# A transformer block with retrieved experts: low parts on two engines in turn, selections cut in four lots, and projections, late rows and row requests reordered

## The reference, cut to what matters

```
px = modulate(rms_norm(x, norm1), sh1, sc1) @ w_in          # 8 chunks of 512 columns; the same for ctx (256 tokens)
x  = x + gt1 * (concat(neighbourhood_attention, hgrn2) @ w_out)
h  = modulate(rms_norm(x, norm2), sh2, sc2)
q  = (h @ wq).reshape(tokens, 8 heads, 2, 128)
s  = einsum(q, sub_keys)                                    # 128 scores for each head and half
s1, i1 = top_k(s[.., 0], 16); s2, i2 = top_k(s[.., 1], 16)
top, pos = top_k(s1[:, None] + s2[None, :], 16)             # the best 16 of 256 pairs
idx = i1 * 128 + i2 at pos;  g = softmax(top)
a   = gelu(u[idx] . h);  out = sum(g * a * v[idx])          # u, v: 16384 rows of 1024
x   = x + gt2 * out
```

## Time and profile before

| | |
|---|---|
| time, median of 3 runs | 2544.76 us (2541.76 to 2547.04) |
| the profiled execution | 2537.28 us, its span 2535.5 us |
| mean granted TensorE clock | 0.967 of full speed |
| PE busy | 2340.6 us, 92% of the span |
| DVE, ACT, POOL busy | 1758.0, 912.2, 620.9 us |
| HBM read, written | 432.60 MB, 52.43 MB |

### The profile page before, as it was taken

How to read it: one execution, slowest core, us unless ns; L and a number is a source line. 1 busy time by engine, 2 the same in 40 slices (tenths; PEclk the granted TensorE clock), 3 DMA queues, 4 the chain that set the end, 5 groups by cost and what they waited for, 6 DMA issues and landing times. The chain is left out here.

```text
span 2535.5 us, 31738 instructions
## 1 busy us (share of the span) xinstructions
PE 2340.6 (92%) x12435; PEld 2041.6 (81%) x12435; DVE 1758.0 (69%) x3152; ACT 912.2 (36%) x1192; POOL 620.9 (24%) x350
## 2 busy tenths in 40 slices
PE   7989888878998998899999799999999899999997
PEld 2768666753788898899999799999999576667775
DVE  6534676761588999799996677778786656654543
ACT  4212234221333233455553232333333434456323
POOL 0000032310344765533333333333330000000000
PEclk9989999889998999999999899999999999999999
DMA  7656310002225666788899999999995222112121
GB/s 258 219 180 207 140 50 1 1 17 100 75 98 192 217 223 205 243 307 324 320 341 360 344 361 354 353 355 353 357 354 188 85 84 66 50 42 67 62 96 67
DMA packets 178245, 489.22 MB, mean 193 GB/s; under 512 B 13712, under 2 KB 80400, under 8 KB 166576
## 3 DMA queue, kind: packets, MB, share of 16 engines
q1 hardware_dynamic: 141232, 352.95, 41.1%
q0 software_dynamic: 36864, 134.23, 13.8%
HBM read 432.60 MB, written 52.43 MB: 191 GB/s over the span
## 5 line engine op out<-in xcount | busy, mean ns | idle before, releaser
L1037 PE MATMUL ps<-h_high,u_high 128*128 128x384 f32 (+1 forms) x1152 | 403.2, 350 | 44.0 <-POOL u_low L1224 33.3
L1038 PE MATMUL ps<-h_low,u_high 128*128 128x384 f32 (+1 forms) x1152 | 396.0, 344 | 0.0
L1039 PE MATMUL ps<-h_high,u_low 128*128 128x384 f32 (+1 forms) x1152 | 395.8, 344 | 0.0
L1037 PE MATMUL ps<-w_high,v_high 128*128 128x384 f32 x1024 | 343.5, 335 | 18.3 <-DVE w_low L1603 18.3
L1038 PE MATMUL ps<-w_low,v_high 128*128 128x384 f32 x1024 | 342.7, 335 | 0.0
L1039 PE MATMUL ps<-w_high,v_low 128*128 128x384 f32 x1024 | 342.6, 335 | 0.0
L1037 PEld LDWEIGHTS ps<-h_high,u_high 128*128 128x128 f32 x1152 | 219.2, 190 | 55.5 <-POOL u_low L1224 36.2
L1037 PE MATMUL ps<-h_high,w_high 128*128 128x512 f32 x568 | 231.7, 408 | 32.0 <-DVE w_low L332 13.3
L1407 ACT ACTIVATE v_high<-v_raw 128x2048 fp32r<-128x2048 f32 x64 | 122.6, 1916 | 351.3 <-PE ps L1039 351.3
L1038 PE MATMUL ps<-h_low,w_high 128*128 128x512 f32 x568 | 225.4, 397 | 0.0
L1039 PE MATMUL ps<-h_high,w_low 128*128 128x512 f32 x568 | 224.7, 396 | 0.0
(11 more groups left out here) (405 smaller groups left out, 4571.8 us busy)
## 6 DMA issues: line engine op xcount, KB each, us to landing
v_raw<-in_peer_v SPq DMA_DIRECT2D x64, 1024.0 KB, 6.5
w_raw<-in_w SPq DMA_DIRECT2D x100, 512.0 KB, 3.5
u_first<-in_uT SPq DMA_DIRECT2D x32, 1024.0 KB, 6.1
u_second<-in_uT SPq DMA_DIRECT2D x32, 1024.0 KB, 6.2
xT<-in_late_w SPq DMA_DIRECT2D x56, 512.0 KB, 4.5
gelu_up<-gelu SPq DMA_DIRECT2D x128, 192.0 KB, 6.8
gates<-gates_sb SPq DMA_DIRECT2D x12, 2048.0 KB, 12.6
weighted<-gelu_up SPq DMA_DIRECT2D x64, 384.0 KB, 6.7
```

Source lines behind the costliest of these rows:

```text
L1037: pe.matmul(out, wh, mh, start=start, stop=False)
L1038: pe.matmul(out, wh, ml, start=False, stop=False)
L1039: return pe.matmul(out, wl, mh, start=False, stop=stop)
```

## The change

It has these parts:

1. Projections, late products: they are spread over steps 2 to 24 (`LATE_FIRST`, `LATE_PIECES`) where it was 0 to 26, two or three in a step, and on DVE stand at the end of their step.
2. The 32 moves of values go out four at a step in steps 12 to 19 (`MOVES`).
3. `high(2)` stands ahead of the row's sigmoid on ACT, `low(2)` ahead of the row's product on DVE.
4. The context scans of the two directions stand in steps 25 and 27, where they were in 25 and 26.
5. Experts, low parts: up to step 43 POOL makes those of even steps g, DVE those of odd steps, at the start of its step. POOL's subtraction stands ahead of the step's row requests and waits until DVE's of the step before is made.
6. `select` is cut in `best_keys`, `best_sums`, `best_pairs` and `key_numbers`. The first two run one step after the unit's scores, the other two a step later still, ahead of the first two of the next unit, and so do the shift, the row numbers and the second shift. ACT's first exponential moves from step 14 to 15.
7. Row requests of u: 44 lots in steps 16 to 43 (before 36), 62 in steps 44 to 67 (before 64), 22 in steps 68 to 75 (before 28). A lot's dot stands one step after its request throughout, where it was two for the first 36.

```diff
--- before.py
+++ after.py
@@ -198,11 +198,12 @@
                 eng.wait_ge(used, part_way[p])
 
 
-        late_pieces = at["in7"] - 1
+        LATE_FIRST, LATE_PIECES, MOVES = 2, 23, 8
 
         def late_at(p):
 
-            return range(min(p, late_pieces) * LATE // late_pieces, min(p + 1, late_pieces) * LATE // late_pieces)
+            first, end = (min(max(q - LATE_FIRST, 0), LATE_PIECES) * LATE // LATE_PIECES for q in (p, p + 1))
+            return range(first, end)
 
         def raw_of(p):
             return k.raws[:, p % RAW1, :] if p < NP - 2 else spare[:, p - NP + 2, :]
@@ -257,11 +258,12 @@
                     late_load(n)
                 if p == at["in6"]:
                     sp.wait_ge(evac, v_last)
-                    for c in range(NCB):
+                if at["in6"] <= p < at["in6"] + MOVES:
+                    first = (p - at["in6"]) * NCB * ROWS // MOVES
+                    for c, r in (divmod(x, ROWS) for x in range(first, first + NCB * ROWS // MOVES)):
                         k0 = min(max(QB * c - KB // 4, 0), GW - KB)
-                        for r in range(ROWS):
-                            sp.dma_start(k.vw[KB * (r % 4):KB * (r % 4) + KB, 2 * c + r // 4, :],
-                                         vnat[GW * (r % 2) + k0:GW * (r % 2) + k0 + KB, r // 2, :]).then_inc(moved, 16)
+                        sp.dma_start(k.vw[KB * (r % 4):KB * (r % 4) + KB, 2 * c + r // 4, :],
+                                     vnat[GW * (r % 2) + k0:GW * (r % 2) + k0 + KB, r // 2, :]).then_inc(moved, 16)
             sp.wait_ge(late_used, LATE)
             sp.dma_start(pred_f, k.dram["pred"].rearrange("p d s t -> p (d s t)")).then_inc(k.preds, 16)
             sp.dma_start(k.mask[:], k.dram["win_mask"]).then_inc(k.table_in, 16)
@@ -336,6 +338,7 @@
             h_lows(k.xT, h_high, h_low, 0, 0)
             low(1)
             h_lows(ctxT, hc_high, hc_low, 1, KT)
+            low(2)
             dve.wait_ge(sg_c, 2)
             dve.tensor_tensor(c_row, c_row, row_gate, ALU.mult).then_inc(silu_c, 1)
             dve.wait_ge(silu_c, 3)
@@ -378,9 +381,7 @@
 
             n = 0
             for p in range(NP):
-                for x in late_at(p):
-                    late_mod(x)
-                if p + 2 < NP:
+                if 2 < p + 2 < NP:
                     low(p + 2)
                 for j in ends[p]:
                     if jobs[j].kind == "silu":
@@ -397,9 +398,11 @@
                     forget_gates(0)
                 if p == f_last + 1:
                     forget_gates(1)
-                if f_last + 1 < p <= f_last + 3:
-                    context_scan(p - f_last - 2)
-                    context_keys(p - f_last - 2)
+                if p in (f_last + 2, f_last + 4):
+                    context_scan((p - f_last) // 2 - 1)
+                    context_keys((p - f_last) // 2 - 1)
+                for x in late_at(p):
+                    late_mod(x)
 
         @block.scalar
         def _(act):
@@ -440,11 +443,12 @@
                     act.wait_ge(scaled, KT * s + t + 1)
                     act.activation(h[:, t, :], y[:, t, :], ACT.Identity, scale=a1[:, t, s:s + 1],
                                    bias=m1[:, t, s:s + 1]).then_inc(modulated, 1)
+            high(2)
             act.wait_ge(rows_in, 16)
             act.activation(row_gate, c_row, ACT.Sigmoid).then_inc(sg_c, 1)
             n = 0
             for p in range(NP):
-                if p + 2 < NP:
+                if 2 < p + 2 < NP:
                     high(p + 2)
                 for j in ends[p]:
                     job = jobs[j]
@@ -1016,14 +1020,19 @@
     return OUT_G + 2 + 2 * u if u < 4 else OUT_G + 10 + 9 * (u - 4) // 4
 
 
+
 def pick_step(n):
 
-    return PICK_AT + 7 * n // 9 if n < 36 else SPREAD_AT + 3 * (n - 36) // 8 if n < 100 else 68 + 2 * (n - 100) // 7
+    if n < 44:
+        return PICK_AT + (SPREAD_AT - PICK_AT) * n // 44
+    if n < 106:
+        return SPREAD_AT + BATCHES // EXPERT_TILES * (n - 44) // 62
+    return GROUPS - 8 + 8 * (n - 106) // 22
 
 
 def dot_step(n):
 
-    return pick_step(n) + (2 if n < 36 else 1)
+    return pick_step(n) + 1
 
 
 def row_step(n):
@@ -1215,14 +1224,16 @@
                     .then_inc(row_in[total % RING], 16)
 
             for x in range(WQ_G + U_G):
+                if x + OUT_G < SPREAD_AT and x % 2 == 0:
+                    pool.wait_ge(u_hi, PIECES_BEFORE + x + 1)
+                    if x:
+                        pool.wait_ge(u_split, PIECES_BEFORE + x)
+                    pool.tensor_tensor(u_low[:, x % 2], u_raw[x % 2][:], u_high[:, x % 2].bitcast(F32),
+                                       ALU.subtract).then_inc(u_split, 1)
                 for n in picks_at[x + OUT_G]:
                     if n == 0:
                         pool.wait_ge(indexed, 1)
                     rows_by_index(n, k.dram["peer_u"], n)
-                if x + OUT_G < SPREAD_AT:
-                    pool.wait_ge(u_hi, PIECES_BEFORE + x + 1)
-                    pool.tensor_tensor(u_low[:, x % 2], u_raw[x % 2][:], u_high[:, x % 2].bitcast(F32),
-                                       ALU.subtract).then_inc(u_split, 1)
             for q in range(U_G):
                 for n in rows_at[q]:
                     rows_by_index(n, k.dram["peer_v"], PICKS + n)
@@ -1366,7 +1377,7 @@
                 if g == OUT_G + 1:
                     act.wait_ge(h_turned, 1)
                     act.activation(h_tok[:], ps[:, 4:6, :].rearrange("p b t -> p (b t)"), ACT.Copy).then_inc(h_tokens, 1)
-                if g == PICK_AT - 2:
+                if g == PICK_AT - 1:
                     act.wait_ge(shifted, 1)
                     act.activation(sel[:, SELF, 2, :], sel[:, SELF, 2, :], ACT.Exp).then_inc(exped, 1)
                 if g == TURN_AT - 2:
@@ -1452,7 +1463,7 @@
             h_lows(KT - 1)
             dve.wait_ge(io_ready, 3)
 
-            def select(u):
+            def best_keys(u):
                 c, tt = unit_of(u)
                 s = s_sb[:, u % 3]
                 dve.wait_ge(s_ready, u + 1)
@@ -1472,6 +1483,8 @@
                 link(last)
                 dve.tensor_copy(indf[:], ind[:])
 
+            def best_sums(u):
+                c, tt = unit_of(u)
                 c4 = cand[:].rearrange("p h (a b) -> p h a b", a=TOPK)
                 link(dve.tensor_tensor(c4, val[:, 0::2, :].unsqueeze(3).to_broadcast([P, UP, TOPK, TOPK]),
                                        val[:, 1::2, :].unsqueeze(2).to_broadcast([P, UP, TOPK, TOPK]), ALU.add))
@@ -1479,6 +1492,10 @@
                 for h in range(UP):
                     last = dve.max(best[:, h, 0:8], cand[:, h, :])
                 link(last)
+
+            def best_pairs(u):
+                c, tt = unit_of(u)
+                best = top[:, tt, c * UP:(c + 1) * UP, :]
                 p3 = pos[:].rearrange("p (h c) -> p h c", h=UP)
                 for h in range(UP):
                     dve.max_index(p3[:, h, 0:8], best[:, h, 0:8], cand[:, h, :])
@@ -1492,6 +1509,9 @@
                 link(last)
                 dve.tensor_scalar(half[:, 0, :], pos[:], 4, None, ALU.logical_shift_right)
                 link(dve.tensor_scalar(half[:, 1, :], pos[:], TOPK - 1, None, ALU.bitwise_and))
+
+            def key_numbers(u):
+                c, tt = unit_of(u)
                 for i in range(2):
                     last = dve.tensor_tensor(pick[:, i], half[:, i, :].unsqueeze(2).to_broadcast([P, UP * TOPK, TOPK]),
                                              io16[:].unsqueeze(1).to_broadcast([P, UP * TOPK, TOPK]), ALU.is_equal)
@@ -1551,18 +1571,22 @@
                 last.then_inc(built, 1)
 
             for g in range(OUT_G, GROUPS):
-                if g >= SPREAD_AT:
+                if g >= SPREAD_AT or (g - OUT_G) % 2:
                     low_u(g - OUT_G)
                 for n in dots_at[g]:
                     dot(n)
-                for u in units_at[g]:
-                    select(u)
+                for u in units_at.get(g - 2, []):
+                    best_pairs(u)
+                    key_numbers(u)
                     if u == per_tile - 1:
                         shift(slice(SELF, TT), 1)
                     if u == per_tile:
                         row_numbers()
                     if u == UNITS - 1:
                         shift(slice(0, SELF), 2)
+                for u in units_at.get(g - 1, []):
+                    best_keys(u)
+                    best_sums(u)
                 if g == TURN_AT - 1:
                     x, inverse = softmax(slice(0, SELF), 2)
                     dve.tensor_tensor(x, x, inverse, ALU.mult).then_inc(selected, 1)
```

## The result

The changed kernel takes 2524.95 us (median of 4 runs, 2523.74 to 2526.2), the kernel before 2543.35 (4 runs, 2541.76 to 2547.04): ratio 0.9926, 95% interval 0.9908 to 0.9943, so 18.4 us less. Forecast were 2534.2 and 10.6 less. The two traces differ by 11.1 (spans 2535.5 and 2524.4), near the forecast. The other 7 are not in any stage of the two traces: the profiled execution of before (2537.3) is 6.1 faster than the median of these runs, that of after (2526.2) 1.3 slower than its own.

What follows compares the result with a forecast made beforehand. PE bounds the kernel nearly everywhere, with DVE nearly as full in the selections; -22.5 (projections) + 19.4 (selections) - 7.5 (spreading and tail) = -10.6, so 2544.8 becomes 2534.2 us, range 2508 to 2560.

Steps and rivals of the forecast that it cites:

- Projections, -22.5: Projection stage: three of PE's waits for weights shrink or go, with the slow clock behind them; 22.5 us won, bounds 15 and 28.
- The second wait: Projections, near 184 us: PE's 12.61 us wait behind SP's run of 32 moves goes whole, plus 1.7 of slow clock.
- The first: Projections, PE's wait of 5.23 us before 68.50: low(2) comes next on DVE, saving 3.5 and about 1.4 of slow clock.
- The third: Projections, PE's 7.94 us wait: only 2.3 go, leaving waits of 2.9 and 2.7 before pieces 27 and 28; 1 of slow clock.
- Selections, +19.4: Expert steps up to 41: DVE's added work and holds start step 41 17.6 us later, plus 1.8 slow clock; 19.4 lost.
- The chain: DVE's work from the row numbers to its low part of step 41, made at about 1047.7 with the holds.
- the first wait at step 19: PE's first and longest wait on DVE's low parts in odd steps, forecast at about 11 us.
- The six holds of 4.5: Second dots in odd steps 17, 25, 27, 29, 31 and 39 stand still during POOL's subtraction: 6 x 4.5 = 27 us.
- The waits for scores, 5 us: DVE's waits for scores in the selection stage, 15.2 us before, shrink to about a third, 5.
- the slow clock: Half clock granted to PE behind a long wait; 1.8 us lost to it in the selections.
- Spreading and tail, -7.5: Steps 44 to 67 give 0; the tail wins 7.5 us from fewer lots and two small waits, bounds 0 and 12.
- the 3.1 MB fewer: Tail: six lots fewer save 3.1 MB, 8 us of DMA at 387 GB/s, of which half was taken as won.

Runs made afterwards that it cites:

- the last experiment section: No edit: the traces compared where no edit reaches; fourteen spread over 7.5 us there, and 44 later runs of the kernel before lie between 2536.0 and 2549.0 us.
- turn about: Low parts on POOL and DVE in turn; the changed kernel with only this undone, POOL making all up to step 43 behind the row requests: 2514.91 us.
- dots last: Changed kernel with DVE's parts of the selection ahead of the step's dots, numbers of dots, low parts and requests kept: 2508.8 us, ratio 0.9869.

## Why the prediction was right, and where it was off

**Projections, -22.5: right, -24.4 measured** by that half alone. The second wait went whole. The first is 1.66 us, where 5.23 less 3.5 makes 1.7. The third left 2.67 and 1.11 where I had 2.9 and 2.7. The waits fell by 20.4, for my 18.4. The last is 1.6 shorter than forecast because PE asked later: behind the wait of 2.67 it ran at half clock and took 7.3 us for its piece (260.62 to 267.96), where I had 5.5.

```profile
261.00:264.50 3.50, 3.50 (x10) 2.69 (x9) 3.09 (x4) 0.00 (x0) 0.00 (x0) 0.54 1.04 428
```

**Selections, +19.4: the right mechanism, and a size that owes something to luck.** By the traces +16.3. For all of the experts' half the medians have +7.9, where the forecast has 19.4 less 7.5, 11.9. The chain named the right engine, and the first wait at step 19, 10.8 us for "about 11"; six dots of over 5 us stand behind DVE's low parts, as the holds had it. Step 41 came 14.1 us later, for 17.6, with errors both ways:

- *The six holds of 4.5* were six of 4.4, at steps 23, 27, 29, 31, 39 and 41 for my 17, 25, 27, 29, 31 and 39. 41's lies behind the low part at which my chain ended, so five counted in it, 22 us for 27. I had looked at the lots of the odd step alone: at 23 no selection follows the single dot, so the two dots of step 24 come up right behind it and the first of them is held; at 25 DVE was not late: POOL waited for ScalarE's copy, and began at 847.3, long after the dots; at 17 it began at 759.7, before the first row was there, and held the first dot. In the earlier trace rows stand two instructions: the first ran its 0.7 us, the second took 5.1, so that hold was 4.4 too.
- *The waits for scores, 5 us, did not come*: DVE had no idle time before its first maximum between 776 and 1011 (15.2 before). On the other side the first dot began at 762.0, 2.7 later than forecast, and two instructions of the selections were held 3.0 and 1.8, the first dot 2.1.
- *A dot costs DVE less than its length.* The next one starts 1.14 us after it (826.26 and 827.40, 832.92 and 834.06), where I had added up 1.22: 3 us less over 38 dots. All these together make some 3.4 us less than forecast at step 41, where 3.5 were measured.
- *The clock was mis-sized.* I priced the slow clock at 1.8 us by the longest wait alone. PE was busy 9.1 us more for the same matmuls, and idle only 7.2 more; 42.1 of waits on low parts in all, just under the 45 to 60 that I gave. Behind five of the shorter waits (at steps 23, 27, 29, 31 and 35, 2.8 to 5.2 us) the clock fell to half as well; I had priced none of these.

**Spreading and tail, -7.5:** 4.7 by the traces. Steps 44 to 67 gave 1.4, for 0, and the rest up to the downward steps 3.3. Of these, some 2.4 are the waits of steps 72 and 73 (1.6 us for 2.3) and the 3.4 us at half clock behind them, which the trace of after lacks; I had 3.5. The wait for the gelu tile in front of the downward steps stayed at 17.7 us (18.3 before), so the 3.1 MB fewer were not what that wait hung on; that half of the term, 4 us, was wrong.

**The total.** The forecast of -10.6 fits the traces (-11.1: -22.7, +16.3, -4.7), where three errors of 0.2, 3.1 and 2.8 us nearly cancel. It misses the medians (-18.4) by 7.8, nearly all of it the 7 us of the last experiment section.

**No step of the sum asked what the turn about is worth alone.** The same lots without it are 10 us faster than the changed kernel, and the same turn about with the dots last another 6.

The Trainium skill, "SBUF — State Buffer", section "Who interferes with whom", says that the ports which VectorE and GpSimd share are an exclusive lock, and that the order of issue decides which of the two blocks. The rows of step 23 agree in both directions: POOL takes 5.42 us for 4.62 behind a dot that runs, and a dot 5.58 for 1.22 behind POOL.

## What to carry to other kernels

When two engines hand work to each other by a semaphore, what follows on the first meets the start of the second: put there instructions that the second one doesn't block (13 us of DVE's time here, for moving one loop below another). Don't put an instruction that waits for a DMA ahead of work that is ready (5.3 us of PE's here). Before moving work to a busy engine, price its waits with the clock that follows each, short ones too. Test the halves of a change alone: here one wins 24 us and hides that the other loses 8.

## What the runs showed of the hardware

- Of DVE's instructions that meet a subtraction of POOL, a dot that already runs is not slowed (1.22 us); the next is held, for 4.4. MAX8, FIND_INDEX8 and MATCH_REPLACE8 keep 0.87, 0.28 and 0.28 us beside it (dots last, 821.4 to 825.9). Besides dots and the selection's products, the shift of positions (TENSOR_SCALAR, 0.2 us alone) was held, up to 4.4 us, and a CAST of indices, up to 3.9.
- The sum of holds says little: in the stage DVE lost 70.5 us to them where POOL made all low parts behind the requests, and 42.8 in the changed kernel, and yet the first kernel is 10 us faster. My reading is that a hold counts where it falls ahead of something that PE waits for.
- The clock fell to half around waits of 3 us too. After the change, around the one of 2.8 us that ended at 826.4 and the one of 5.2 that ended at 915.4 (the second row holds 2.2 us of that wait):

```profile
827.90:831.30 3.40, 3.40 (x12) 3.40 (x12) 3.40 (x1) 0.00 (x0) 3.40 (x1) 0.50 0.79 294
...
913.20:920.00 6.80, 4.58 (x14) 4.58 (x15) 6.80 (x4) 0.00 (x0) 4.49 (x1) 0.50 0.48 143
```

In the trace of before it did so behind a wait of 2.3 us that ended at 879.5, and not behind waits of 2.5 (851.1) and 2.7 (919.1):

```profile
880.30:883.70 3.40, 3.40 (x12) 3.40 (x11) 3.29 (x14) 0.00 (x0) 3.38 (x2) 0.50 0.94 258
...
919.10:923.10 4.00, 4.00 (x23) 4.00 (x24) 3.86 (x15) 0.00 (x0) 3.87 (x2) 1.00 0.74 199
```
